# A hybrid decoder layer: the residual x transposed on TensorE from the copy already on chip, a reordered front, and half of the low parts of one normalised input computed on GpSimd

## Chip, cores and metric

The kernel runs on one core of one Trainium2 chip. The metric is the device time of one execution in microseconds (us), as the median over several executions. A core has five engines that run side by side and wait for one another only through semaphores: TensorE (PE in the profile), VectorE (DVE), ScalarE (ACT), GpSimd (POOL) and SyncE (SP). Sixteen DMA engines move data between the memory of the chip (HBM) and the buffers on the core.

## What is computed

One inference step of one layer, for a prompt of 256 tokens and for 8 single sample tokens (264 token columns in all), with model width 2048:

```
n1 = rmsnorm(x) ; [q | f | v | g | u] = n1 @ w_in            # 2048 -> 5120
o  = rmsnorm(hgrn2(q, f, v)) * silu(g)                       # 8 heads, state 128x128
pm = multiscale_pool(u) @ w_pool
h  = x + [o | pm] @ w_out                                    # the residual x is added here
h  = h + (silu(gate) * up) @ w_down                          # FFN on rmsnorm(h) @ w_gate_up, width 5632
h  = h + sigmoid(h @ w_ple_gate) * rmsnorm(p @ w_ple)
y  = rmsnorm(h)
```

The new recurrent states and the last 15 pooling inputs are outputs as well. All is float32.

## The kernel before

Activations are kept with features on the 128 partitions and the 264 tokens along the row, one tile of 128x264 for each 128 features (`KT = 16` tiles for the width). Each float32 operand of a product is split into two float16 parts, high and low, and each 128x128 piece of weights is multiplied three times: high by high, high by low, low by high (lines 1415, 1417 and 1419, in `stream`). A weight **block** is 512 KB, two tiles of 128 input features by 512 outputs. For each block SyncE issues the load into one of four `raw` buffers when the block four before it has been split (`load`, line 410, waiting for `lo_done`), ScalarE makes the high part (`split`, line 531), VectorE the low part (line 798), and TensorE runs 24 matmuls over it. The order on every engine is written out by hand by block number `b`. The input projection is blocks 0 to 79 in ten groups of eight; each group ends with the eviction of four accumulator tiles (`evict_in`, lines 540, 950, 951 and 955), and TensorE may write a tile of the next group only when `acc_free` says that it was evicted.

Small products and transposes are **jobs**: a numbered list `JOBS` in which each uses the next of four PSUM banks (`wrk`), and `job(name)` makes TensorE wait until the job four before it has been taken out (`drained`). Their instructions are woven between the matmuls of a block.

**The front.** x is loaded token by token (`x_tok`, two loads of 1 MB by SyncE, semaphores `x_in`), the sample rows `x_smp` and the identity matrix `ident` by ScalarE's queue. TensorE runs matmuls on zeros (`idle_matmuls`, line 1442, their counts in `IDLE_MMS`), transposes the sample rows (line 1450), sums their squares (`xq`, line 1456), transposes the gain vectors (`vec`, line 1459), and transposes the scaled x (`n1_k`, lines 1468 and 1470). VectorE sums half of the squares of each x tile (`half_squares`, line 854), takes the sample results (lines 859 to 861), forms the reciprocal roots (lines 864 to 869, 816 to 818) and scales x (line 888).

**The residual x.** The features-on-partitions copy of x, needed in `h_all` when the output projection begins, comes from a second load of x: 32 loads of 64 KB by GpSimd's queue (line 504), paced by `lo_done`, into `x_blk`, and eight VectorE 32x32 block transposes of 128x512 (line 1218) in blocks 33 to 40. GpSimd also loads the recurrent states (line 471, from `lo_done` 8 on), the pooling buffer, and fills scratch with zeros (lines 493 to 496).

**Before the FFN.** When h is complete, VectorE forms each of the 16 tiles of the normalised h (line 1239, `ntmp`, four temporaries), ScalarE its high part (line 732), and VectorE its low part (line 1246). VectorE then waits in tile k for the low part of tile k - 4. The FFN follows in 22 groups of 8 blocks. ScalarE splits blocks 4 to 7 of the FFN's group 0 and 0 to 3 of group 1 after the last high part, and evicts group 0 (line 540) after these.

## Time and profile before

| | |
|---|---|
| median of 3 executions | 1227.67 us (1224.66 to 1231.83) |
| profiled execution: its own time, its span | 1222.89 us, 1221.1 us |
| TensorE busy in the span | 1196.5 us (98%) |
| VectorE, ScalarE, GpSimd busy | 793.4 us, 589.5 us, 48.7 us |
| mean granted TensorE clock | 0.992 of full speed |
| HBM traffic | 192 GB/s over the span |

Times in the rows are us from the start of the span. A matmul's row tells its latency; matmuls overlap, so the rate is read from the distance of their starts. In a timeline row the square brackets tell how long the engine had been idle and which instruction's end released it. A granted clock of 1.00 is 2.4 GHz, one of 0.50 is 1.2 GHz.

### The profile page before, as it was taken

To read this page: it belongs to the slowest core of one execution; us is meant where nothing else is said; L and a number is where in the kernel's file an instruction comes from. 1 tells how busy PE (TensorE), PEld (TensorE's weight loads), DVE (VectorE), ACT (ScalarE), POOL (GpSimd) and SP (SyncE) were. 2 spreads that over 40 slices of the span, in tenths; PEclk is the share of its full clock that TensorE was granted. 3 is DMA by queue.
4 is the path that set the end of the run, shared out by engine and by line. 5 is a ranking of instruction groups with operands and counts; after the bars stand their busy time and mean duration, and the time that the engine had idled before them with its cause. 6 is when DMAs were issued, how large, how long until landed. Compare 5 with 4: busy or idle time off the path is not lost.

```text
span 1221.1 us, 27627 instructions
## 1 busy us (share of the span) xinstructions
PE 1196.5 (98%) x10779; PEld 1042.5 (85%) x10779; DVE 793.4 (65%) x1169; ACT 589.5 (48%) x727; POOL 48.7 (4%) x73
## 2 busy tenths in 40 slices
PE   7999999999999899999999999999999999999996
PEld 6888989888888788888888888888888888888885
DVE  6677787678868865665656556565664645454786
ACT  5543533555546745555545554555453434343442
POOL 2430110100000000000000000000000000000000
PEclk8999999999999999999999999999999999999998
DMA  7885765766555566575665757657464646565551
GB/s 236 247 247 143 238 182 167 222 183 202 176 204 191 172 194 219 158 222 170 210 202 170 222 158 223 189 182 226 142 242 144 235 159 221 172 221 184 189 162 72
DMA packets 173336, 234.98 MB, mean 192 GB/s; under 512 B 10690, under 2 KB 111273, under 8 KB 173000
## 3 DMA queue, kind: packets, MB, share of 16 engines
q1 hardware_dynamic: 167728, 220.30, 55.9%
q0 software_dynamic: 4048, 12.19, 3.6%
q10 hardware_dynamic: 1504, 1.70, 0.4%
q8 instruction: 39, 0.64, 0.2%
q14 instruction: 17, 0.14, 0.0%
HBM read 227.18 MB, written 7.43 MB: 192 GB/s over the span
## 4 chain that ended last, share of the span: by engine, by line
PE 88%; DVE 6%; DMA 3%; ACT 2%; issue 2%; ACTq 0%; SPq 0%; DVEq 0%
PE acc L1415 28%; PE acc L1419 28%; PE acc L1417 28%; DVE lo L798 2%; PE wrk L1561 2%; DMA raw<-in_w_in_dram 1%; ACT hi L531 1%; DMA ident<-in_c_ident_dram 1%; DMA raw<-in_w_gate_up_dram 0%; PE wrk L1442 0%; DVE nrm L1246 0%; DMA raw<-in_w_out_dram 0%; DVE a L1239 0%; DVE tg L1239 0%; PE wrk L1768 0%
## 5 line engine op out<-in xcount | busy, mean ns | idle before, releaser
L1415 PE MATMUL acc<-nrm,hi 128*128 128x264 f16 x2304 | 636.7, 276 | 7.1 <-DVE tg L1252 2.6
L1417 PE MATMUL acc<-nrm,hi 128*128 128x264 f16 x2304 | 636.7, 276 | 0.0
L1419 PE MATMUL acc<-nrm,lo 128*128 128x264 f16 x2304 | 636.6, 276 | 0.0
L798 DVE SCALAR_TENSOR_TENSOR lo<-raw,hi 128x1024 f16<-128x1024 f32 x414 | 497.1, 1221 | 213.2 <-ACT hi L531 209.5
L531 ACT ACTIVATE hi<-raw 128x1024 f16<-128x1024 f32 x414 | 424.1, 1051 | 327.6 <-DMA raw<-in_w_gate_up_dram 105.7
L1415 PEld LDWEIGHTS acc<-nrm,hi 128*128 128x128 f16 x2304 | 227.4, 99 | 41.4 <-DVE tg L1252 2.9
L1419 PEld LDWEIGHTS acc<-nrm,lo 128*128 128x128 f16 x2304 | 228.4, 99 | 32.7
L1417 PEld LDWEIGHTS acc<-nrm,hi 128*128 128x128 f16 x2304 | 228.4, 99 | 32.6
L1415 PE MATMUL acc<-big,hi 128*128 128x264 f16 x720 | 198.7, 276 | 0.0
L1417 PE MATMUL acc<-big,hi 128*128 128x264 f16 x720 | 198.7, 276 | 0.0
L1419 PE MATMUL acc<-big,lo 128*128 128x264 f16 x720 | 198.7, 276 | 0.0
L540 ACT ACTIVATE gate_t<-acc 128x264 f32<-128x264 f32 x84 | 32.7, 391 | 154.9 <-PE acc L1419 154.9
L1252 DVE SCALAR_TENSOR_TENSOR tg<-acc,gate_t 128x264 f32<-128x264 f32 x44 | 19.0, 433 | 111.8 <-ACT gate_t L540 111.8
L1417 PEld LDWEIGHTS acc<-big,hi 128*128 128x128 f16 x720 | 70.5, 98 | 10.7
L1415 PEld LDWEIGHTS acc<-big,hi 128*128 128x128 f16 x720 | 70.5, 98 | 10.6
L1419 PEld LDWEIGHTS acc<-big,lo 128*128 128x128 f16 x720 | 70.5, 98 | 10.5
L1415 PE MATMUL acc<-mix,hi 128*128 128x264 f16 x256 | 70.6, 276 | 1.1 <-DVE mix L1129 0.7
L1419 PE MATMUL acc<-mix,lo 128*128 128x264 f16 x256 | 70.7, 276 | 0.0
L1417 PE MATMUL acc<-mix,hi 128*128 128x264 f16 x256 | 70.7, 276 | 0.0
L1561 PE MATMUL wrk<-big 128*128 128x64 f32 x224 | 32.2, 247 | 0.6 <-DVE mix L1014 0.6
L1561 PEld LDWEIGHTS wrk<-big 128*128 128x128 f32 x224 | 31.7, 190 | 1.1 <-DVE mix L1014 0.9
L1415 PEld LDWEIGHTS acc<-mix,hi 128*128 128x128 f16 x256 | 25.0, 98 | 5.4 <-DVE lo L798 1.0
(287 smaller groups left out, 747.4 us busy)
## 6 DMA issues: line engine op xcount, KB each, us to landing
raw<-in_w_gate_up_dram SPq DMA_DIRECT2D x352, 256.0 KB, 3.8
raw<-in_w_down_dram SPq DMA_DIRECT2D x88, 512.0 KB, 4.7
raw<-in_w_in_dram SPq DMA_DIRECT2D x80, 512.0 KB, 4.5
raw<-in_w_out_dram SPq DMA_DIRECT2D x32, 512.0 KB, 4.4
raw<-in_w_ple_gate_dram SPq DMA_DIRECT2D x32, 512.0 KB, 4.7
state<-in_state_hgrn_dram POOLq DMA_DIRECT2D x8, 512.0 KB, 6.1
out_new_hgrn_sample_dram<-state POOLq DMA_DIRECT2D x8, 512.0 KB, 5.2
xe<-in_x_prompt_dram SPq DMA_DIRECT2D x2, 1024.0 KB, 6.9
```

Source lines behind the costliest of these rows:

```text
L531: nc.scalar.activation(hi[:, st.hl_slot(j), :], raw[:, st.raw_slot(j), :], ACT.Copy, scale=WSCALE).then_inc(hi_done, 1)
L540: nc.scalar.activation(gate_t[:, n, :], acc[:, n, 0:TOK], ACT.Sigmoid, scale=c).then_inc(gate_ready, 1)
L798: stt(lo[:, st.hl_slot(j), :], raw[:, st.raw_slot(j), :], WSCALE, hi[:, st.hl_slot(j), :], ALU.mult, ALU.subtract).then_inc(lo_done, 1)
L1252: stt(tg32[:, n, :], acc[:, n, 0:TOK], C_FFN, gate_t[:, n, :], ALU.mult, ALU.mult).then_inc(acc_free, 1)
L1415: mm(out, wh, x_hi[:, kt, :], start=first, stop=False)
L1417: mm(out, wh, x_lo[:, kt, :], start=False, stop=False)
L1419: last = mm(out, wl, x_hi[:, kt, :], start=False, stop=final)
L1561: last = mm(out[:, n * 64:(n + 1) * 64].rearrange("p (n k) -> p n k", k=1 << l), k, right, start=True, stop=True)
```

## The change

Three edits are made together. First, the second load of x and the VectorE transposes are removed; TensorE transposes `x_tok` in blocks 8 to 15 (jobs `xt_0` to `xt_15`, two 128x128 transposes each), and ScalarE copies each 128x256 result into `h_all`. The buffers on top of `x_tok` may be filled only after the last of these, so GpSimd's load of the pooling buffer and its memsets now wait for `xt_15` in place of `n1_15`. Second, in the front, ScalarE's queue issues the load of `ident` ahead of that of `x_smp`, which is written without the split into four columns, and the counts of the matmuls on zeros are 26, 4, 0 and 12 where they were 24, 16, 8 and 16. Third, the low parts of the odd tiles before the FFN are made by GpSimd, which signals `n_odd`; VectorE keeps the even ones.

```diff
-X_TURN_AT, X_LOAD_AT, PT_AT, CONST_AT = 33, 4, 16, 4
+X_AT, PT_AT, CONST_AT = 8, 16, 4
-IDLE_MMS = (24, 16, 8, 16)
+IDLE_MMS = (26, 4, 0, 12)
...
+    if _b in range(X_AT, X_AT + KT // 2):
+        JOBS += [(f"xt_{2 * (_b - X_AT) + _n}", "act") for _n in range(2)]
...
-            pool.wait_ge(drained["dve"], drain_of(f"n1_{KT - 1}")[1])
+            pool.wait_ge(drained["act"], drain_of(f"xt_{KT - 1}")[1])
             pool.dma_start(buf_tok, io["state_pool"][0].rearrange("b j c -> (b j) c")).then_inc(buf_in, 16)
...
-            pool.wait_ge(masks_ready, 1)
-            for m in range(SEQ // 32):
-                for q in range(4):
-                    if q % 2 == 0:
-                        pool.wait_ge(lo_done, X_LOAD_AT + AHEAD + 2 * m + q // 2)
-                    src = io["x_prompt"][0, 32 * m:32 * m + 32, :].rearrange("r (k q f) -> r k q f", q=4, f=32)
-                    pool.dma_start(x_blk[32 * q:32 * q + 32, :, 32 * m:32 * m + 32], src[:, :, q, :]).then_inc(x_blk_in, 16)
...
+            for k in range(1, KT, 2):
+                pool.wait_ge(n_hi_ready, KT + k + 1)
+                pool.wait_ge(xn_ready, X_SCALED + k + 1)
+                nc.gpsimd.tensor_tensor(n_lo[:, k, :], ntmp(k), n_hi[:, k, :], ALU.subtract).then_inc(n_odd, 1)
...
-            act.dma_start(x_smp.rearrange("b (c d) -> b c d", c=4), io["x_sample"][:, 0, :].rearrange("b (c d) -> b c d", c=4))\
-                .then_inc(x_in[2], 16)
             act.dma_start(ident[:], io["c_ident"]).then_inc(id_in, 16)
+            act.dma_start(x_smp, io["x_sample"][:, 0, :]).then_inc(x_in[2], 16)
...
+            def x_tile(k):
+                wait_job(f"xt_{k}")
+                nc.scalar.activation(h_all[:, k, 0:SEQ], wrk[:, JOB[f"xt_{k}"] % JOB_BANKS, 0:SEQ], ACT.Copy)\
+                    .then_inc(drained["act"], 1)
...
                 if b + AHEAD > len(EARLY_SPLITS):
                     split(*MIX_BLOCKS[b + AHEAD])
+                if b in range(X_AT, X_AT + KT // 2):
+                    for n in range(2):
+                        x_tile(2 * (b - X_AT) + n)
...
-                if b in range(X_TURN_AT, X_TURN_AT + KT // 2):
-                    ks = slice(2 * (b - X_TURN_AT), 2 * (b - X_TURN_AT) + 2)
-                    dve.wait_ge(x_blk_in, 16 * 4 * (SEQ // 32))
-                    nc.vector.transpose(h_all[:, ks, 0:SEQ], x_blk[:, ks, :]).then_inc(x_ready, 1)
...
                     if k >= 4:
-                        dve.wait_ge(n_ready, k - 3)
+                        dve.wait_ge(n_odd if k % 2 else n_ready, k // 2 - 1)
...
-                if k >= 2:
+                if k >= 2 and k % 2 == 0:
                     dve.wait_ge(n_hi_ready, KT + k - 1)
                     tt(n_lo[:, k - 2, :], ntmp(k - 2), n_hi[:, k - 2, :], ALU.subtract).then_inc(n_ready, 1)
...
+            def x_features(k):
+
+                out = job(f"xt_{k}")
+                nc.tensor.transpose(out[:, 0:P], x_tok[:, 0, k * P:(k + 1) * P], ident[:])
+                yield
+                nc.tensor.transpose(out[:, P:SEQ], x_tok[:, 1, k * P:(k + 1) * P], ident[:]).then_inc(job_done, 1)
+                yield
...
-                stream(S_FFN, i, n_hi, n_lo, ready=lambda j: pe.wait_ge(n_ready, 2 * j + 2))
+                stream(S_FFN, i, n_hi, n_lo, ready=ffn_ready)
```

On TensorE, the start of the program, before (`hi` holds the zeros of the matmuls that do no work, `xe` the sample rows, `mix` the sums of squares, `big` the gain vectors):

```order
L1442 MATMUL wrk<-hi 128x264 x24
L1450 MATMUL wrk<-ident,xe 128x8 x16
L1442 MATMUL wrk<-hi 128x264 x16
L1456 MATMUL wrk<-mix,ones 128x8
L1442 MATMUL wrk<-hi 128x264 x8
L1459 MATMUL wrk<-ident,big 128x81
L1442 MATMUL wrk<-hi 128x264 x16
```

and the same place in the changed program:

```order
L1443 MATMUL wrk<-hi 128x264 x26
L1451 MATMUL wrk<-ident,xe 128x8 x16
L1443 MATMUL wrk<-hi 128x264 x4
L1457 MATMUL wrk<-mix,ones 128x8
L1460 MATMUL wrk<-ident,big 128x81
L1443 MATMUL wrk<-hi 128x264 x12
```

The matmuls on zeros ahead of the sums of squares went from 16 to 4, those ahead of the vectors from 8 to none.

On TensorE, the start of block 8 in the changed program (before, the same place is matmuls of lines 1415, 1417 and 1419 alone):

```order
L1416 MATMUL acc<-nrm,hi 128x264
L1699 MATMUL wrk<-ident,xe 128x128
L1418 MATMUL acc<-nrm,hi 128x264
L1701 MATMUL wrk<-ident,xe 128x128
L1420 MATMUL acc<-nrm,lo 128x264
L1699 MATMUL wrk<-ident,xe 128x128
L1416 MATMUL acc<-nrm,hi 128x264
L1701 MATMUL wrk<-ident,xe 128x128
```

Four transposes of x were woven into the block; each of blocks 8 to 15 has four.

On VectorE, the tiles from 8 on before the FFN (`a` and `tg` are the temporaries, `nrm` the low parts; `lo<-raw,hi` is the split of a weight block), before:

```order
L798 SCALAR_TENSOR_TENSOR lo<-raw,hi 128x1024
L1239 SCALAR_TENSOR_TENSOR a<-hid,gf,wrk 128x264
L1246 TENSOR_TENSOR nrm<-tg,nrm 128x264
L1239 SCALAR_TENSOR_TENSOR a<-hid,gf,wrk 128x264
L1246 TENSOR_TENSOR nrm<-tg,nrm 128x264
L1239 SCALAR_TENSOR_TENSOR tg<-hid,gf,wrk 128x264
L1246 TENSOR_TENSOR nrm<-a,nrm 128x264
L1239 SCALAR_TENSOR_TENSOR tg<-hid,gf,wrk 128x264
L1246 TENSOR_TENSOR nrm<-a,nrm 128x264
```

and in the changed program:

```order
L803 SCALAR_TENSOR_TENSOR lo<-raw,hi 128x1024
L1240 SCALAR_TENSOR_TENSOR a<-hid,gf,wrk 128x264
L1247 TENSOR_TENSOR nrm<-tg,nrm 128x264
L1240 SCALAR_TENSOR_TENSOR a<-hid,gf,wrk 128x264
L1240 SCALAR_TENSOR_TENSOR tg<-hid,gf,wrk 128x264
L1247 TENSOR_TENSOR nrm<-a,nrm 128x264
L1240 SCALAR_TENSOR_TENSOR tg<-hid,gf,wrk 128x264
```

For each two tiles one subtraction has left VectorE; eight stand at the end of GpSimd's program.

## Rows read from the trace of the kernel before

**Rows 1.** The page, busy time of each engine.
```profile
PE 1196.5 (98%) x10779; PEld 1042.5 (85%) x10779; DVE 793.4 (65%) x1169; ACT 589.5 (48%) x727; POOL 48.7 (4%) x73
```

**Rows 2.** Waits of TensorE, whole span: us in total, times, longest us.
```profile
PE acc L1415 <- DVE tg L1252: 2.6, 1, 2.6
PE acc L1415 <- DVE big L955: 1.6, 1, 1.6
...
PE wrk L1561 <- DVE mix L1014: 0.6, 1, 0.6
...
PE acc L1415 <- DVE big L951: 0.5, 1, 0.5
```

**Rows 3.** Timeline of the front: start us, us, engine, line, operation.
```profile
9.27 1.87 PE L1450 MATMUL wrk<-ident,xe 8*128 8x8 f32 x16 [3.69 <-DMA ident<-in_c_ident_dram]
9.41 1.06 ACT L569 ACTIVATE big<-xe 128x1024 f32<-128x1024 f32 x1 [1.88 <-DMA xe<-in_x_prompt_dram]
...
11.07 3.70 PE L1442 MATMUL wrk<-hi 128*128 128x264 f16 x16
...
12.20 1.21 DVE L854 CUSTOM_DVE_ANT_0 big<-xe 128x1024 f32<-128x1024 f32 x1
...
15.03 0.17 DVE L864 TENSOR_SCALAR gate_t<-wrk 128x8 f32<-128x8 f32 x1 [1.61 <-PE wrk L1456]
...
17.37 0.49 DVE L888 TENSOR_SCALAR big<-xe,gate_t 128x512 f32<-128x512 f32 x1
```

**Rows 4.** DMA queue of ScalarE (q10) from 0 to 2.5, then from 5 to 6.
```profile
q10 hardware_dynamic: 7, 0.06, 10.1%
...
q10 hardware_dynamic: 27, 0.01, 4.6%
```

**Rows 5.** Window: stretch, length, busy PE PEld DVE ACT POOL, PEclk, DMA share, GB/s.
```profile
45.00:50.00 5.00, 3.39 (x31) 2.77 (x29) 3.86 (x7) 1.34 (x2) 4.72 (x9) 1.00 1.02 308
```

**Rows 6.** Timeline of TensorE inside block 1, woven transposes.
```profile
24.33 0.27 PE L1470 MATMUL wrk<-ident,big 128*128 128x128 f32 x1
...
24.44 0.28 PE L1419 MATMUL acc<-nrm,lo 128*128 128x264 f16 x1
```

**Rows 7.** Timeline of GpSimd, VectorE and ScalarE, 40 to 54 us.
```profile
40.90 0.97 POOL L493 MEMSET mix<- 128x1024 f32 x1
41.79 1.83 POOL L494 MEMSET xe<- 128x2048 f16 x1
...
41.16 0.17 DVE L921 TENSOR_TENSOR lbt<-lbt 128x8 f32<-128x8 f32 x1
41.36 2.41 DVE L922 TENSOR_SCALAR lbt<-lbt 128x8 f32<-128x8 f32 x1
...
44.01 2.36 DVE L798 SCALAR_TENSOR_TENSOR lo<-raw,hi 128x1024 f16<-128x1024 f32 x2
...
53.11 1.06 ACT L531 ACTIVATE hi<-raw 128x1024 f16<-128x1024 f32 x1 [6.50 <-DMA raw<-in_w_in_dram]
```

**Rows 8.** Timeline of VectorE near 162 us.
```profile
162.36 0.70 DVE L1218 STREAM_TRANSPOSE hid<-big 128x512 f32<-128x512 f32 x1
```

**Rows 9.** Timeline of VectorE, then ScalarE, before the FFN.
```profile
400.75 0.48 DVE L1239 SCALAR_TENSOR_TENSOR a<-hid,gf,wrk 128x264 f32<-128x264 f32 x1
401.15 0.42 DVE L1246 TENSOR_TENSOR nrm<-tg,nrm 128x264 f16<-128x264 f32 x1
...
405.95 0.48 DVE L1239 SCALAR_TENSOR_TENSOR tg<-hid,gf,wrk 128x264 f32<-128x264 f32 x1
...
393.69 0.82 ACT L732 ACTIVATE nrm<-a 128x264 f16<-128x264 f32 x2 [0.88 <-DVE a L1239]
...
408.20 3.90 ACT L531 ACTIVATE hi<-raw 128x1024 f16<-128x1024 f32 x4
```

**Rows 10.** Windows at the change from FFN group 0 to 1.
```profile
424.00:425.00 1.00, 0.82 (x5) 0.59 (x6) 0.86 (x4) 1.00 (x1) 0.00 (x0) 0.65 0.82 251
...
427.00:428.00 1.00, 1.00 (x8) 0.72 (x7) 1.00 (x2) 1.00 (x2) 0.00 (x0) 0.65 0.24 84
```

More of the change, by code:

```diff
@@ L268, in build @@
         e_sq, e_ssq = mix[:, 0:TOK], mix[:, TOK:2 * TOK]
-        x_blk = big[:, 4 * HEADS * TOK:4 * HEADS * TOK + KT * SEQ].rearrange("p (k t) -> p k t", t=SEQ)
         y_tok = big[:, 0:2 * D].rearrange("p (a d) -> p a d", a=2)
@@ L348, in build @@
         xs_ready, ns_hi = sem("xs_ready"), sem("ns_hi")
-        x_blk_in, masks_ready, x_ready = sem("x_blk_in"), sem("masks_ready"), sem("x_ready")
         sq_ready, mean_ready, rstd_ready, xn_ready = sem("sq_ready"), sem("mean_ready"), sem("rstd_ready"), sem("xn_ready")
-        n_hi_ready, n_ready = sem("n_hi_ready"), sem("n_ready")
+        n_hi_ready, n_ready, n_odd = sem("n_hi_ready"), sem("n_ready"), sem("n_odd")
         q16_ready, s_hi_ready, s_lo_ready = sem("q16_ready"), sem("s_hi_ready"), sem("s_lo_ready")
@@ L917, in constants @@
                 nc.vector.tensor_copy(ident16[:], ident[:])
-                nc.vector.tensor_copy(masks[:], masks_f).then_inc(masks_ready, 1)
+                link(nc.vector.tensor_copy(masks[:], masks_f))
                 link(nc.vector.reciprocal(lbt[:, 2, :], lbt[:, 1, :]))
@@ L1151, in _ @@
                     if st is S_OUT_O[0]:
-                        dve.wait_ge(x_ready, KT // 2)
+                        dve.wait_ge(drained["act"], drain_of(f"xt_{KT - 1}")[1])
                     out_tiles(st, S_OUT_O.index(st))
@@ L1698, in in_jobs @@
                     yield from ple_features()
+                if b in range(X_AT, X_AT + KT // 2):
+                    for n in range(2):
+                        yield from x_features(2 * (b - X_AT) + n)
                 for c in range(QUADS):
@@ L1753, in _, with ffn_ready @@
             stream(S_PLE, 0, pt_hi, pt_lo, ready=sum_h, layout=lambda j, n, kk: (kk * COLS + n * P, kk))
+            def ffn_ready(j):
+                pe.wait_ge(n_ready, j + 1)
+                pe.wait_ge(n_odd, j + 1)
             with pe.Fori(0, S_FFN.groups) as i:
-                stream(S_FFN, i, n_hi, n_lo, ready=lambda j: pe.wait_ge(n_ready, 2 * j + 2))
+                stream(S_FFN, i, n_hi, n_lo, ready=ffn_ready)
             out = job("es")
@@ L1776, in y_transposes @@
                 yield
-            stream(S_GATE, 0, n_hi, n_lo, ready=lambda j: pe.wait_ge(n_ready, KT + 2 * j + 2))
+            stream(S_GATE, 0, n_hi, n_lo, ready=lambda j: pe.wait_ge(n_ready, KT // 2 + 2 * j + 2))
             with pe.Fori(1, S_GATE.groups - 1) as i:
```

## Prediction

> **What bounds the kernel now.** I read the page first: TensorE is busy 98% of the span [rows 1], so a change is worth only what it adds to TensorE's work or takes from its few waits, and what the clock does around them. Then the list of TensorE's waits: apart from the front, those that this change can touch are 2.6 us at the end of the FFN's first group, 1.6 and 0.5 us at the ends of the first two groups of the input projection, and 0.6 us at the second diagonal [rows 2]. The timeline of the front shows where the first 17 us go, and windows show the granted clock.
>
> The front: TensorE waits 3.69 us for the identity matrix and starts the sample transposes at 9.27; the 16 matmuls on zeros behind them take 3.70 us, 0.23 each where one of the same shape takes 0.11 later [rows 6], which is the lower clock, so that VectorE, done with its squares at 13.41, waits 1.61 us for the sums of squares and starts its chain at 15.03; x is scaled from 17.37 on [rows 3].
>
> The first group change: a VectorE instruction on 8 columns took 2.41 us, from 41.36 to 43.77, until a GpSimd memset of 1.83 us (41.79 to 43.62) had ended; the two weight splits behind it ran until 46.37 and the evictions that TensorE waited for came after them [rows 7].
>
> The FFN: the last product tile starts at 405.95, ScalarE starts the four splits of group 0 at 408.20, everything behind them is late, TensorE waits 2.6 us for the first eviction [rows 9, 2], and the clock is at its lower level behind it. A mean of 0.65 is 0.3 at full speed and 0.7 at half, so from 424.3 to 427.7, 3.4 us [rows 10].
>
> **The change part by part.** All terms are in us against the profiled execution, 1222.9 (span 1221.1). It lies 4.8 below the median of the three timed runs, 1227.67; I take the difference over unchanged.
>
> *Transposes of x on TensorE.* 32 instructions. In block 1 the same kind, woven, starts 0.11 before the matmul behind it [rows 6], so each takes one slot of 0.11: 32 x 0.11 = **+3.5**. No wait hides them, since the block loop runs without a gap. Their 16 copies on ScalarE are 128x256 from PSUM; two tiles of 128x264 take it 0.82 from SBUF [rows 9], so about 6.6 in some 25 us in which ScalarE idles up to 6.5 at a time [rows 7]: nothing. What is queued behind a copy is the split of the block five ahead, with four blocks of 2.7 us in hand.
>
> *The second load and VectorE's transposes go.* ScalarE sat 6.50 idle for a weight block that landed at 53.11 [rows 7], with states, pooling buffer, x and weights on the DMA engines at once. Without x, and with the pooling buffer and memsets put behind block 15, the 2.41 us instruction should take what its neighbours take (about 0.2), and both splits and evictions move up by 2.2, more than the 1.6 of wait: **-1.6**. The 0.5 of the second group change is late by a weight block that lands late: **-0.5**. The 0.6 at the diagonal ends a fully occupied stretch of VectorE in which block transposes of 0.70 stand, the last at 162.36 [rows 8]; two of them make 1.3: **-0.6**. Zero to 2.7 is the bound of the three together. GpSimd's buffer loads and memsets now start about 2 us after the last copy, near 70, and its zeros are first needed in block 18, near 74. If VectorE meets the memset again there, it costs it up to 2.2, in a place where it has two blocks (5.3) in hand: nothing.
>
> *The front.* Four matmuls on zeros in place of 16 take 0.9 (3.70 / 16 x 4) and end at about 12.0, ahead of VectorE. So VectorE's chain starts when its squares are done, at 13.41: -1.6. That is the lower bound. The upper one comes from the identity matrix. It was issued at 1.39, second in its queue, and landed at 9.27. Of that queue 7 packets with nearly all of the 64 KB of sample rows had moved by 2.5 us, while the small packets of the identity move only after 5 [rows 4]: what was issued first went at once, what came second waited behind the first 1 MB of x. Issued first it should land near 6.5, and the sample rows (8 packets) near 7. Then the sample work is over before the second half of x lands at 9.41 [rows 3], VectorE's squares run 9.41 to 10.6 instead of 12.20 to 13.41, nothing waits, and scaling starts at 17.37 - 1.61 - 2.8 = 13.0: -4.4. Against this stands the clock. With fewer matmuls on zeros TensorE has little to do between the last of them and the first weight block: eight transposes, one microsecond with a gap on each side. Before, it was down after 3.69 of idle time [rows 3]. If it falls here at the first block and stays at 1.2 GHz for 3.4 us, as after 424 [rows 10], that costs 1.7, and twice that if it stays twice as long. Of 4.4 I keep **-3.1**.
>
> *The low parts.* From product to low part VectorE takes 0.40, and the seven pairs from tile 8's product to tile 15's 5.20, 0.74 each, so a low part is 0.34 [rows 9]. Two tiles took 1.48, now 1.14. Up to tile 8 ScalarE's splits set the pace (I find 0.3 to gain there). From tile 8 to the end of tile 15, 400.75 to 406.35, the 5.6 become 8 x 0.40 + 4 x 0.34 = 4.6. Together **-1.4** on ScalarE's last high part, on the four splits behind it, and on loads, gates and evictions that follow from them. TensorE's wait becomes 1.2 of 2.6. The wait of 1.6 at the first group change left the clock at full speed [rows 5], and that of 2.6 did not: I expect the fall to go. It cost half of the 3.4 us: **-1.7**. GpSimd's subtraction of 128x264 is in no row. Its memset moves 2048 columns in 1.83 [rows 7], 0.24 for 264; one pass for each operand and the result gives 0.7. Between 0.24 and that I take 0.7. It has 1.14 for each tile and two tiles of slack through `ntmp`, so VectorE does not wait for it.
>
> The Trainium skill (GPSIMD Engine Reference, Performance versus the Vector engine) gives 4497 ns for this operation on 2048 columns; by that figure a tile is an estimated 0.58, and the sum would be the same.
>
> **Sum.** 3.5 - 1.6 - 0.5 - 0.6 - 3.1 - 1.4 - 1.7 = -5.4. That is 1217.5 in the profiled execution's terms, **1222.3** as a median, 0.44% faster. 0.5% (6.1 us) is about what a measurement of this kernel can tell from no change.
>
> **The rivals.**
>
> *A. The clock holds in the front.* Then the front gives its 4.4 and the sum is -6.7: 1221.0, faster. For it: the wait of 1.6 at 45 to 47 did not lower the clock [rows 5]. Against it: two gaps follow each other closely here.
>
> *B. The identity does not land earlier,* because both loads share the DMA engines with 2 MB of x. The front gives 1.6, the sum is -3.9: 1223.8. The packets of [rows 4] speak against it.
>
> *C. GpSimd and VectorE hold each other up.* The instruction that ended with the memset [rows 7] shows that it can happen. VectorE would then do its own 4.6 plus four subtractions of 0.7 where 5.6 stood: 1.8 later instead of 1.4 earlier, with the clock's fall kept, so -5.4 + 3.2 + 1.7: 1227.2, no change. Against it: the instruction just before the one held up, a two-input one at 41.16, took 0.17 while another memset ran, from 40.90 to 41.87 [rows 7].
>
> By the Trainium skill (GPSIMD Engine Reference, Specifications) contention is to be expected with VectorE instructions that have two SBUF inputs, as line 1246 and the weight split have. The 0.17 us neighbour does not agree with that, though it is a short one and a memset reads nothing.
>
> *D. The DMA engines stay behind,* as the states alone keep weight blocks late. ScalarE's copies stand behind a split that waits for the block four ahead, so TensorE would meet full banks from block 10 on: block 12 landed at 53.1 and TensorE would want the first bank back near 52. The waits of 1.6 and 0.5 become others of that size and one or two us are added: -5.4 + 2.1 + 1.5 = -1.8, 1225.9.
>
> *E. Slower: GpSimd is the bound before the FFN.* VectorE's tile 15 needs GpSimd's low part of tile 11, its sixth, and the first can begin at about 394.1, when ScalarE has made the first two high parts [rows 9]. With T for one, tile 15 starts no earlier than 394.1 + 6 T. It is level with before (405.95) at T = 2.0; the rest of the sum (-2.3) is eaten up at T = 2.4, and from 3.4 on the kernel is 6 us slower: 1234. That is five times my 0.7.
>
> **How the numbers follow.** My forecast has 0.46, A 0.19, B 0.10, C 0.09, D 0.07, E and anything like it 0.09. Within the forecast the clock's cost in the front may be anything between its two levels, 1.2 to each side, so 0.4 of it lies beyond 6.1 us. Faster: 0.19 + 0.4 x 0.46 = 0.37, with what is left of noise in the median 0.39. Slower: E, 0.09. Within 0.5%: 0.52. The range goes from A less the uncertainty of the median (the three runs lie 7 apart, so their median may be off by 2 to 3) at 1218 to a little beyond C at 1229. The forecast's own is 1220 to 1225.
>
> **What would show it.** The sample transposes start at or before 7.5 instead of 9.27; VectorE's x scaling near 13; no TensorE wait at the first two group changes and none near 167; the block loop from 8 to 15 longer by 3.5; GpSimd's subtractions under 1.1 apart; ScalarE's four splits near 1.4 earlier relative to the first product tile; a wait near 1.2 at the end of FFN group 0 with the clock at 1.00 behind it. I am wrong if the identity lands at 9 again, if VectorE waits for `n_odd`, if a fall of the clock at the first weight blocks eats the front, or if TensorE waits on full banks in blocks 10 to 15.

## The result, and the profile after

| | before | changed |
|---|---|---|
| median | 1226.81 us (5 runs, 1222.43 to 1231.83) | 1218.66 us (5 runs, 1217.32 to 1219.73) |
| ratio of the times, 95% interval | | 0.9939 (0.991 to 0.9969) |
| profiled execution: time, span | 1222.89, 1221.1 us | 1218.66, 1216.9 us |

The medians lie 8.1 us apart; the measured ratio of the times is 0.9939, 0.61% or 7.5 us faster. The two profiled executions differ by only 4.2 us of span, and much of what follows is about the other 4. The page, busy time, answers to [rows 1]: TensorE 3.0 us more, VectorE 8.1 and GpSimd 14.9 less.

```profile
PE 1199.5 (99%) x10789; PEld 1045.2 (86%) x10789; DVE 785.3 (65%) x1153; ACT 594.0 (49%) x743; POOL 33.8 (3%) x49
```

TensorE's waits (total, times, longest), to be held against [rows 2]: 2.6 has become 1.1, and the two group changes and the diagonal have left the list. In the front the sample rows have taken the identity's place.

```profile
PE wrk L1451 <- DMA xe<-in_x_sample_dram: 1.8, 1, 1.8
PE acc L1416 <- DVE tg L1253: 1.1, 1, 1.1
```

Timeline of the front of the changed kernel (start, us, engine, line, operation, idle before), beside [rows 3]:

```profile
7.72 1.06 ACT L566 ACTIVATE big<-xe 128x1024 f32<-128x1024 f32 x1 [4.43 <-DMA xe<-in_x_prompt_dram]
8.06 1.30 PE L1451 MATMUL wrk<-ident,xe 8*128 8x8 f32 x16 [1.79 <-DMA xe<-in_x_sample_dram]
10.19 1.06 ACT L566 ACTIVATE big<-xe 128x1024 f32<-128x1024 f32 x1 [1.31 <-DMA xe<-in_x_prompt_dram]
13.84 0.49 DVE L893 TENSOR_SCALAR big<-xe,gate_t 128x512 f32<-128x512 f32 x1
17.39 0.38 PE L1416 MATMUL acc<-nrm,hi 128*128 128x264 f16 x1 [0.74 <-DVE nrm L915]
```

x is scaled 3.5 earlier (17.37 to 13.84), although its halves arrive later (10.19 against 9.41). The windows of the same execution (length, busy PE PEld DVE ACT POOL, granted clock, DMA share, GB/s) show the price: TensorE, idle from about 6.3 to 8.06, drops to the lower clock near the end of the window 8 to 9 and stays there for over 13 us, through the first weight blocks.

```profile
8.00:9.00 1.00, 0.94 (x14) 0.97 (x15) 1.00 (x2) 0.87 (x2) 0.00 (x0) 0.90 0.98 363
...
10.00:16.00 6.00, 5.08 (x23) 3.57 (x22) 5.55 (x19) 4.47 (x9) 2.94 (x5) 0.50 1.05 374
16.00:22.00 6.00, 5.26 (x26) 3.65 (x25) 5.96 (x12) 5.82 (x10) 0.00 (x0) 0.50 0.67 189
22.00:23.00 1.00, 1.00 (x9) 0.78 (x8) 1.00 (x1) 0.00 (x0) 0.00 (x0) 0.77 0.71 182
```

The first group change, beside [rows 7]: the instruction on 8 columns takes 0.17 where it took 2.41, and ScalarE's copies of x (line 662) run between the splits.

```profile
40.47 0.17 DVE L927 TENSOR_SCALAR lbt<-lbt 128x8 f32<-128x8 f32 x1
...
40.88 2.36 DVE L803 SCALAR_TENSOR_TENSOR lo<-raw,hi 128x1024 f16<-128x1024 f32 x2
...
47.02 0.64 ACT L662 ACTIVATE hid<-wrk 128x256 f32<-128x256 f32 x2
```

Before the FFN, beside [rows 9]: GpSimd's subtractions, 1.14 apart with 0.39 idle between them; VectorE beside them; ScalarE's four splits, at 406.05 where they were at 408.20.

```profile
401.38 0.75 POOL L518 TENSOR_TENSOR nrm<-a,nrm 128x264 f16<-128x264 f32 x1 [0.39 <-ACT nrm L737]
402.52 0.76 POOL L518 TENSOR_TENSOR nrm<-tg,nrm 128x264 f16<-128x264 f32 x1 [0.39 <-ACT nrm L737]
...
401.51 0.48 DVE L1240 SCALAR_TENSOR_TENSOR tg<-hid,gf,wrk 128x264 f32<-128x264 f32 x1
401.91 0.48 DVE L1240 SCALAR_TENSOR_TENSOR a<-hid,gf,wrk 128x264 f32<-128x264 f32 x1
402.31 0.42 DVE L1247 TENSOR_TENSOR nrm<-tg,nrm 128x264 f16<-128x264 f32 x1
402.65 0.48 DVE L1240 SCALAR_TENSOR_TENSOR a<-hid,gf,wrk 128x264 f32<-128x264 f32 x1
...
406.05 3.90 ACT L529 ACTIVATE hi<-raw 128x1024 f16<-128x1024 f32 x4
```

Windows behind FFN group 0, of the changed kernel: the clock holds.

```profile
420.00:425.00 5.00, 3.88 (x35) 3.14 (x34) 4.08 (x8) 4.96 (x7) 0.00 (x0) 1.00 0.84 267
425.00:430.00 5.00, 5.00 (x47) 4.36 (x45) 4.72 (x6) 2.44 (x3) 0.00 (x0) 1.00 0.58 162
```

The same two windows of the kernel before had 0.93 and 0.73:

```profile
420.00:425.00 5.00, 2.37 (x19) 1.69 (x18) 3.94 (x7) 4.58 (x6) 0.00 (x0) 0.93 0.72 213
425.00:430.00 5.00, 5.00 (x34) 3.82 (x33) 4.70 (x7) 4.24 (x5) 0.00 (x0) 0.73 0.54 169
```

Three stretches between fixed points of TensorE's program carry all the rest. They are read from one profiled execution of each kernel, as the starts of the first weight matmul of block 8, of the first of block 24, and of the very last weight matmul; "waits" are TensorE's at the first and second group change, and "clock" tells whether the granted clock fell behind the second, with what that cost. The experiments that are described below are in it too.

| execution | to block 8 | block 8 to 24 | block 24 to last | waits | clock |
|---|---|---|---|---|---|
| before, first profile | 46.9 | 50.4 | 1110.5 | 1.6, 0.5 | held |
| before, second profile (12) | 47.3 | 55.1 | 1110.0 | 1.6, 3.5 | fell, 1.7 |
| 1, front alone | 42.7 | 54.3 | 1109.8 | 1.6, 2.6 | fell, 1.7 |
| 2, x on TensorE alone | 45.7 | 53.3 | 1109.3 | 0, 0 | held |
| 3, odd low parts alone | 46.2 | 52.0 | 1107.0 | 1.6, 2.1 | held |
| 8, before, memsets later | 46.9 | 55.4 | 1108.2 | 0, 3.5 | fell, 1.7 |
| changed, first profile | 44.1 | 53.3 | 1106.3 | 0, 0 | held |
| changed, second profile (5) | 41.0 | 53.3 | 1106.7 | 0, 0 | held |
| 9, changed, x loaded as well | 42.8 | 53.3 | 1106.0 | 0, 0 | held |
| 11, changed, no odd low parts | 42.5 | 53.3 | 1109.4 | 0, 0 | held |

The table's points are worked out by counting matmuls on `acc`, eight blocks being 192 of them. The last column is read from windows of the clock. Three of them, of 70 to 80 us, are of the kernel before (first profile), of its second profile, and of experiment 8; 0.83 of ten microseconds is 3.4 us at half speed, 1.7 us of work lost:

```profile
70.00:80.00 10.00, 10.00 (x91) 8.81 (x89) 8.20 (x12) 5.24 (x5) 3.15 (x5) 1.00 0.89 254
...
70.00:80.00 10.00, 7.40 (x52) 5.95 (x53) 7.82 (x15) 5.78 (x9) 3.91 (x6) 0.83 0.92 239
...
70.00:80.00 10.00, 7.38 (x52) 6.17 (x53) 8.20 (x16) 4.94 (x9) 5.35 (x9) 0.83 0.99 259
```

Experiment 1 has 0.94 in 60 to 70 and 0.89 in 70 to 80, again 1.7 lost. With this the middle column adds up for the kernels without the transposes: 50.4, plus what the wait exceeds 0.5 by, plus 1.7 where the clock fell, gives 55.1, 54.2, 52.0 and 55.1 where 55.1, 54.3, 52.0 and 55.4 were measured (experiment 8 has one more wait there, of 0.2).

### The profile page after: what moved, and what is told of

The parts are those of the page before. It is cut to its first block, busy times and chain, and to the rows that moved or that the text cites. A ratio compares the mean times of both kernels' runs of the same rounds, so it can differ in the third digit from the quotient of the medians.

```text
span 1216.9 us, 27632 instructions
## 1 busy us (share of the span) xinstructions
PE 1199.5 (99%) x10789; PEld 1045.2 (86%) x10789; DVE 785.3 (65%) x1153; ACT 594.0 (49%) x743; POOL 33.8 (3%) x49
## 4 chain that ended last, share of the span: by engine, by line
PE 94%; DVE 2%; ACT 1%; DMA 1%; issue 1%; ACTq 0%; SPq 0%; DVEq 0%
PE acc L1416 30%; PE acc L1418 30%; PE acc L1420 30%; PE wrk L1562 2%; DVE lo L803 1%; DMA raw<-in_w_gate_up_dram 1%; ACT hi L529 1%; DMA xe<-in_x_sample_dram 1%; PE wrk L1547 0%; DVE a L1240 0%; PE wrk L1536 0%; PE wrk L1785 0%; PE wrk L1691 0%; ACT big L773 0%; PE wrk L1511 0%
```

## The experiments

The first four were compared on one chip (kernel before: 1224.53, 28 runs), 5 to 8 on another occasion (1224.80, 15 runs), 9 to 12 on a third (1223.91, 13 runs).

**1 to 3: each part of the change alone.** The edits are the diff of the change in three pieces.

```diff
-IDLE_MMS = (24, 16, 8, 16)                          # 1: with the order of the two loads
+IDLE_MMS = (26, 4, 0, 12)
...
+    if _b in range(X_AT, X_AT + KT // 2):            # 2: with everything of xt_* and x_blk
+        JOBS += [(f"xt_{2 * (_b - X_AT) + _n}", "act") for _n in range(2)]
...
+            for k in range(1, KT, 2):                # 3: with everything of n_odd
```

> The kernel before with the front's edit alone (order of the two loads on ScalarE's queue, 26, 4, 0 and 12 matmuls on zeros). Theory 1 (the first weight matmul comes about 3.4 us earlier, and the clock, at its lower level until about 22 us, takes some 2.2 of it back): first weight matmul near 17.4, block 8 reached 1.0 to 1.3 us earlier than before. Rival (the front does nothing, all of the 8 us between the medians comes from elsewhere): block 8 at the same time as before. Second rival (with a clock that happens to hold, the front is worth its 3.4): block 8 3.4 earlier. Medians: 1.2 faster, 0, 3.4 faster.

Measured: 1220.56 (1217.46 to 1222.17, 11 runs), ratio 0.9964 (0.9949 to 0.9979), by the ratio 4.4 us faster. In its profile the sample transposes start at 7.47 and block 8 comes 4.2 earlier than before. The clock was at 0.50 from 11 to 14 only, and full before the first weight matmul:

```profile
10.00:11.00 1.00, 0.58 (x4) 0.47 (x5) 1.00 (x1) 1.00 (x2) 0.79 (x2) 0.85 1.05 387
11.00:14.00 3.00, 2.67 (x13) 1.52 (x10) 2.69 (x15) 2.05 (x6) 2.16 (x4) 0.50 1.05 387
14.00:15.00 1.00, 0.94 (x8) 0.88 (x8) 1.00 (x2) 1.00 (x3) 0.00 (x0) 0.94 1.08 402
```

Theory 1 had the clock wrong; the second rival, block 8 3.4 earlier, came nearest. Part of it was lost again in this execution: the wait at the second group change was 2.6, and the clock fell behind it.

> The kernel before with the transposes of x on TensorE and without the second load, nothing else of the change. Theory 1 (a trade that is level): +3.5 for 32 transposes, -1.6, -0.5, -0.6 and some tenths for waits that go: 0.5 to 0.8 us slower to no change in one profile. Rival (the second load costs more in most executions than in the profiled one of before, where executions lie 9 us apart, and its absence is where the narrow spread of the changed kernel comes from): 3 to 5 us faster in the median and a spread under 3 us.

Measured: 1222.40 (1220.99 to 1223.85, 11 runs), ratio 0.9988 (0.9976 to 0.9999). Both group waits and the diagonal's are gone, 3.3 us of transposes are there, and the wait of 2.1 at the FFN still brings a clock of 0.66 in 425 to 430. The gain lies between theory and rival. What stands out is the spread: 2.9 us over 11 runs, where experiments 1 and 3, which keep the second load, spread over 4.7 and 5.3 in 11, and the kernel before over 7.4 in 28.

> The kernel before with the odd low parts on GpSimd alone. Theory 1: ScalarE's last high part 1.4 us earlier against the first product, with the wait at the end of the FFN's first group near 1.2 us instead of 2.6 and no fall of the clock behind it: 3.1 to 3.4 us faster, in the profile and in the median. Rival (the fall of the clock behind that wait is chance, and would have been absent anyway): 1.4 faster in the median.

Measured: 1221.73 (1220.23 to 1225.51, 11 runs), ratio 0.9988 (0.9974 to 1.0002); the last stretch of the table is 3.5 shorter than before, the FFN wait 0.5, the clock 1.00 behind it. So this profile bears out the theory, but the ratio, 1.5 us with an interval from none to 3.2, does not tell its 3.1 to 3.4 from the rival's 1.4; experiment 11 is the better evidence. By the ratios the three savings, 4.4 + 1.5 + 1.5 = 7.4, add up to the 0.61% that the whole change saved, within an uncertainty of 1.4 to 1.8 each.

**4 to 7: the clock and the order in the front.** All are the changed kernel; 4, 6 and 7 run more matmuls on zeros, so that TensorE has no long gap. 5 is the changed kernel once more.

```diff
-IDLE_MMS = (26, 4, 0, 12)
+IDLE_MMS = (42, 12, 0, 26)                          # 4, 6, 7
...
             act.dma_start(x_smp, ...)               # 6: ahead of ident again
             sp.dma_start(ident[:], io["c_ident"])   # 7: on SyncE's queue, ahead of x
```

> The changed kernel with 42, 12, 0 and 26 matmuls on zeros in place of 26, 4, 0 and 12, so that TensorE has work in all of the front. Theory 1 (idle time in the front lets the clock fall, and that costs 2.2 us of the first weight blocks): clock at 1.00 from 5 us on, first weight matmul near 17.4 or some tenths later, block 8 2 us earlier than in the changed kernel, median 2 us faster. Rival (the clock falls whatever TensorE does there): same clock, the additional zeros at the lower rate run until 16 to 17 us and push the first weight matmul 1 to 2 us later.

Measured: 1216.77 (1215.85 to 1218.21, 6 runs), ratio 0.9942 (0.9918 to 0.9967). The clock is 1.00 in all of the front, the first weight matmul starts at 16.6 and block 8 at 41.0, 3.0 earlier than in the changed kernel's first profile. In the front the theory came out; what the zeros are worth is seen only against experiment 5.

> The changed kernel as it is, on the same chip as the next three. Theory 1: it repeats 1217 to 1220 us, and lies 2 us above the kernel with more matmuls on zeros (1216.8) where the clock falls in the front. Rival (the difference between the two is one of chips): both within 0.5 us.

Measured: 1215.97 (1215.71 to 1216.29, 5 runs), ratio 0.9934 (0.992 to 0.9947). The theory missed: experiment 4 is not 2 us faster than this. The same program has block 8 at 41.0 without any extra zeros. In this execution the clock fell just as before, but came back at 15 and not at 22.5:

```profile
8.00:9.00 1.00, 1.00 (x13) 0.93 (x13) 0.65 (x2) 0.44 (x2) 0.00 (x0) 0.66 0.93 350
9.00:14.00 5.00, 4.37 (x19) 2.59 (x17) 4.62 (x18) 3.13 (x6) 2.94 (x5) 0.50 1.05 385
...
15.00:16.00 1.00, 0.64 (x5) 0.40 (x3) 0.89 (x3) 1.00 (x3) 0.00 (x0) 0.93 0.96 279
16.00:24.00 8.00, 7.27 (x65) 6.55 (x66) 7.96 (x14) 7.15 (x13) 0.00 (x0) 1.00 0.74 211
```

From the first weight matmul to block 8 it is 24.3 us here and 26.7 in the first profile. So the price of the clock in the front is not a constant of the program: 2.4 us in one execution, nothing in another. Experiments 10 and 11, with the same front, had it at 0.50 until just before 20 and took 25.8 to 25.9. Experiment 9 had it back at 14 and lost it again from 17.3 to 20.7, just behind its first weight matmul, and took 26.0.

> The changed kernel with 42, 12, 0 and 26 matmuls on zeros, and the sample rows loaded ahead of the identity again, as before. Theory 1 (what is issued second waits behind the first half of x, so the order is worth the time from the sample rows' landing near 7.1 to 8.1 to that of the identity near 9.3): sample transposes at 9.3 and scaling of x at 14.5 to 15.8 instead of 13 to 13.8, 1.5 to 2.5 us slower than with the identity first. Rival (VectorE's squares of the second half of x set the time in either order, and that half lands earlier, near 9.1, when the sample rows are first): under 0.5 us between them.

Measured: 1218.22 (1217.73 to 1219.22, 5 runs), ratio 0.9954 (0.994 to 0.9968), 2.2 over experiment 5 and 2.0 over experiment 7, with ranges that don't touch. The order of the two loads, with the sample rows written in four columns again, is all that sets it apart from experiment 4, which ran on another chip: by the ratios 1.5 us, and block 8 at 42.8 against 41.0. The identity, second in its queue, landed at 9.62, and x was scaled at 15.06:

```profile
9.62 1.15 PE L1452 MATMUL wrk<-ident,xe 8*128 8x8 f32 x16 [1.39 <-DMA ident<-in_c_ident_dram]
...
15.06 0.49 DVE L894 TENSOR_SCALAR big<-xe,gate_t 128x512 f32<-128x512 f32 x1
```

> The changed kernel with 42, 12, 0 and 26 matmuls on zeros, the identity issued by SyncE ahead of x, and the sample rows by ScalarE: neither comes second in a queue. Theory 1 (each queue's first load goes at once): sample transposes near 6.5, second half of x 0.4 us later than otherwise, scaling of x from 12.5 to 13.5, that is 0 to 1 us earlier than with both on ScalarE's queue. Rival (a load of 128 small packets ahead of x holds up x itself): halves of x 1 us later or more, and the kernel slower by that.

Measured: 1216.23 (1215.85 to 1216.91, 5 runs), ratio 0.9937 (0.9923 to 0.995): level with experiment 5. Its clock was 1.00 in all of the front and x was scaled at 13.00, though the sample transposes started at 7.50, right behind the zeros, and not at 6.5. Yet no gain over the unchanged program shows; whether extra zeros pay on a chip whose clock comes back late wasn't compared.

**8: the kernel before with its memsets some 5 us later.**

```diff
+            pool.wait_ge(lo_done, 11)
             nc.gpsimd.memset(scores[:, 0:2], 0.0)
```

> The kernel before, with GpSimd's memsets waiting for the low part of weight block 10, so that they no longer run beside VectorE's constants; the second load of x follows them. Theory 1 (the memset holds up the VectorE instruction of 2.41 us and so the evictions): that instruction takes 0.2 us, and the wait of 1.6 us at the first group change is gone. Rival (the DMA traffic of the second load of x causes it): the wait stays. The second group change keeps its wait of 0.5 to 2.6 us in either case, since weight blocks land late.

Measured: 1225.86 (1223.34 to 1228.58, 10 runs), ratio 1.0012 (0.9998 to 1.0025). The wait at the first group change is gone and the 8-column instruction takes 0.17, so the memset was its cause; the second load can't be, as its first transfer is issued behind the memsets in the kernel before (43.66). The time didn't follow, for two reasons that this one execution shows. The clock, full in that place in the kernel before, fell behind the first weight matmul (0.66, 0.50, 0.50 and 0.64 in the four windows from 21 to 25, 1.7 us lost), so that block 8 came at 46.9 as before; and the second change cost its wait of 3.5 and a second fall. Whether either goes with the moved memsets was not tested. VectorE's evictions and splits ran at their usual 0.43 and 1.23 beside the moved memset (the split only for its first 0.3 us):

```profile
46.93 1.81 POOL L495 MEMSET xe<- 128x2048 f16 x1
...
43.20 0.17 DVE L923 TENSOR_SCALAR lbt<-lbt 128x8 f32<-128x8 f32 x1
...
47.55 0.43 DVE L956 SCALAR_TENSOR_TENSOR big<-acc,gate_t 128x264 f32<-128x264 f32 x1 [0.24 <-ACT gate_t L541]
48.49 1.23 DVE L799 SCALAR_TENSOR_TENSOR lo<-raw,hi 128x1024 f16<-128x1024 f32 x1 [0.51 <-ACT hi L532]
```

**9: the changed kernel with the blocked load of x put back.** The loaded copy isn't used.

```diff
+            pool.wait_ge(masks_ready, 1)
+            for m in range(0, 6):                   # and 6, 7 behind the memsets
...
+                    pool.dma_start(x_blk[...], src[:, :, q, :]).then_inc(x_blk_in, 16)
```

> The changed kernel with the 32 transfers of the second, blocked load of x put back on GpSimd's queue, gated as before; the transposes stay on TensorE and the loaded copy of x isn't used. Theory (the second load costs through the DMA engines, which then have no time to spare between 50 and 80 us, so that the weight blocks come late): the DMA share of the stretches 50:60 and 60:70 rises from 0.79 and 0.39 to about 1.0, TensorE waits again at the second group change by 0.5 to 3.5 us (the four kernels with that load waited 0.5, 2.6, 2.1 and 4.0 there), and block 8 to block 24 takes 54 to 57 us instead of 53.3; the median is 1 to 3 us over the changed kernel's 1216 to 1218.7. Rival (the waits at the group changes came of the order on VectorE and ScalarE, or of GpSimd's memsets alone, and not of the load): no wait there, 53.3 us from block 8 to block 24, no change within 0.5 us.

Measured: 1216.77 (1215.4 to 1218.46, 4 runs), ratio 0.9947 (0.9929 to 0.9964). The expectation's wait of 4.0 for experiment 8 should read 3.5. My theory was half wrong. The DMA engines did fill up (1.02 in 50 to 60, 0.97 in 60 to 70), and weight blocks took longer from issue to landing. This is the DMA view of 44 to 72 us, its last column the median us to landing; first the changed kernel:

```profile
raw<-in_w_in_dram SPq DMA_DIRECT2D x9, 512.0 KB, 4.4
```

then experiment 9:

```profile
raw<-in_w_in_dram SPq DMA_DIRECT2D x9, 512.0 KB, 7.6
big<-in_x_prompt_dram POOLq DMA_DIRECT2D x16, 64.0 KB, 5.9
```

and the kernel before, second profile:

```profile
raw<-in_w_in_dram SPq DMA_DIRECT2D x10, 512.0 KB, 9.5
big<-in_x_prompt_dram POOLq DMA_DIRECT2D x22, 64.0 KB, 6.7
```

But TensorE didn't wait, and block 8 to 24 took the same 53.3. Late weights alone don't make the wait. The first profile of the kernel before had 8.8 in this view and waited 0.5, experiment 1 had 7.9 and waited 2.6. The likely reason why experiment 9 with its 7.6 waited for nothing is that TensorE, with 3.3 us of transposes in blocks 8 to 15, came to each block later. That is an inference: weights were also less late here than in any of the five executions of the other kernels with that load (7.9 to 9.5), and the memsets lay elsewhere.

**10 and 11: GpSimd's share before the FFN,** three times over, and none.

```diff
+                for _ in range(2):                  # 10: ahead of the subtraction that counts
+                    links += 1
+                    nc.gpsimd.tensor_tensor(n_lo[:, k, :], ntmp(k), n_hi[:, k, :], ALU.subtract).then_inc(n_rep, 1)
+                    pool.wait_ge(n_rep, links)
...
-            for k in range(1, KT, 2):               # 11: with everything of n_odd
```

> The changed kernel with each of GpSimd's eight subtractions done three times over, one after the other, so that its step is about 2.3 us and the distance between two of its tiles about 3.4 instead of 1.14 us where it is busy throughout. Rival E of the prediction (GpSimd the bound): the last of the eight ends near 393.8 + 7 x 3.4 + 2.3 = 420 instead of 405.5, the wait ahead of FFN group 1 grows from 1.1 to 10 us or more or waits appear within group 0, the clock falls behind it, and the kernel is 8 us or more slower than the changed one. If FFN group 0 takes the tiles as slowly as they come (21.6 us for 16 tiles, an odd one each 2.7 us), much of it is hidden: 2 to 5 us slower. Rival (VectorE's eight remaining subtractions and the products set the pace, GpSimd has room): the time stays within 1 us.

Measured: 1222.10 (1220.97 to 1223.5, 10 runs), ratio 0.9988 (0.9976 to 0.9999). From tile 7 to tile 13 a step of three took 2.24 us and steps followed one another without a gap, so the distance was 2.24, not my 3.4; a step that met a weight split of VectorE's took 3.1. VectorE now stood idle 0.58 in each pair of tiles for GpSimd, and TensorE met a weight block that wasn't split, 3.9 us, with the clock at 0.83 in 410 to 420:

```profile
407.50 0.49 DVE L1246 SCALAR_TENSOR_TENSOR tg<-hid,gf,wrk 128x264 f32<-128x264 f32 x1 [0.58 <-POOL nrm L524]
...
412.51 0.40 PE L1422 MATMUL acc<-nrm,hi 128*128 128x264 f16 x1 [3.91 <-DVE lo L809]
```

By the ratios this is 5 to 6.6 us over the changed kernel (0.9947 of experiment 9, 0.9934 of 5), between the two figures I had given, and about level with the kernel before.

The profile of this experiment also shows what the changed kernel's doesn't: the two engines do hold each other up. The first two are GpSimd's passes, one that met a split and one beside which VectorE did nothing; the others are VectorE's split and subtraction beside passes of GpSimd.

```profile
393.65 1.55 POOL L524 TENSOR_TENSOR nrm<-a,nrm 128x264 f16<-128x264 f32 x1
...
409.28 0.68 POOL L524 TENSOR_TENSOR nrm<-a,nrm 128x264 f16<-128x264 f32 x1
...
392.96 1.70 DVE L809 SCALAR_TENSOR_TENSOR lo<-raw,hi 128x1024 f16<-128x1024 f32 x1 [0.30 <-ACT hi L535]
...
396.21 0.88 DVE L1253 TENSOR_TENSOR nrm<-a,nrm 128x264 f16<-128x264 f32 x1
```

The split takes 1.23 alone and the subtraction 0.37 to 0.42. Four subtractions took 0.85 to 0.88, three passes 1.55. So part of what this experiment cost is contention, and not GpSimd's rate alone.

> The changed kernel with all 16 low parts back on VectorE. Theory: the wait ahead of FFN group 1 is 2.1 to 2.6 us instead of 1.1, the clock falls behind it as in the kernel before (0.65 to 0.93 in stretches of 5 us), and the kernel takes 2.5 to 3.5 us more than the changed one. Rival (the odd low parts gave the wait of 1.4 us alone, and the clock's fall hung on something else): 1.0 to 1.6 us more, with the clock at 1.00 behind the wait.

Measured: 1218.78 (1216.44 to 1219.99, 4 runs), ratio 0.9956 (0.994 to 0.9973). The wait is 2.4 and the clock 0.78 and 0.88 behind it; the last stretch of the table is 2.7 to 3.4 longer than with the odd low parts. Theory right.

```profile
420.00:425.00 5.00, 3.46 (x22) 2.61 (x23) 4.08 (x8) 4.96 (x7) 0.00 (x0) 0.78 0.85 258
425.00:430.00 5.00, 5.00 (x41) 4.16 (x40) 4.58 (x6) 2.51 (x3) 0.00 (x0) 0.88 0.66 189
```

**12: the kernel before, unchanged, a second profile.**

> The kernel before, unchanged, for a second profile. Theory (the second load of x leaves the DMA engines no room, so that what lands last at the second group change differs from one execution to the next): the wait at the second group change isn't 0.5 again but somewhere in 0.5 to 3.5 us, while the wait at the first (1.6, set by the memset beside VectorE's small operation) and the one behind FFN group 0 (2.6) come back within 0.1. Rival: all three come back within 0.1, and the spread of the kernel's time comes from elsewhere.

Measured: this execution took 1227.57, its span 1225.7, 4.6 over the first profile. The waits are 3.5, 1.6 and 2.8 (second change, first change, FFN; the last 0.2 over its first value and not within 0.1). ScalarE stood idle 3.29 for a block of weights, and VectorE's gates came behind its split; the lines are of ScalarE, VectorE and TensorE:

```profile
69.48 1.06 ACT L531 ACTIVATE hi<-raw 128x1024 f16<-128x1024 f32 x1 [3.29 <-DMA raw<-in_w_in_dram]
...
70.57 1.23 DVE L798 SCALAR_TENSOR_TENSOR lo<-raw,hi 128x1024 f16<-128x1024 f32 x1 [3.12 <-ACT hi L531]
...
72.60 0.27 PE L1415 MATMUL acc<-nrm,hi 128*128 128x264 f16 x1 [3.54 <-DVE big L951]
```

Block 8 to 24 took 55.1 instead of 50.4: 4.6 again, so this one stretch holds the whole difference between the two executions of the same program. The wait makes 3.0 of it and the clock, which fell behind it, the other 1.7.

## Why the prediction was right, and where it wasn't

The range held the time, though only just: 1218.7 lies 0.7 above its lower end and below the forecast's own 1220 to 1225. At 0.61% the change is past the line of 0.5%, a side to which the prediction gave 0.39 against 0.52 for staying within it. The mechanisms of the likeliest case were all there, one of them badly undersized. The sum of -5.4 was set against the profiled execution; there it came to -4.2. (The low parts, 1.04 and 0.3, make 1.3 and not 1.4; nothing hangs on it.) Term by term:

| term | predicted | first profiles | what the runs add |
|---|---|---|---|
| transposes on TensorE | +3.5 | +3.3 | the same in nine executions |
| first group change | -1.6 | -1.6 | 8: the memset was its cause |
| second group change | -0.5 | -0.5 | waits of 2.1 to 3.5 in four other executions, with 1.7 of clock in three of them |
| diagonal | -0.6 | -0.6 | |
| front | -3.1 | -1.2 | -4.2 in experiment 1; the clock takes 0 to 2.4 back |
| low parts | -1.4 | -1.5 | |
| clock behind FFN group 0 | -1.7 | -1.7 | 11: both together 2.7 to 3.4 |

In the third column the front is the stretch to block 8 less the 1.6 of wait. The low parts are the FFN's wait, 2.6 to 1.1; the clock is what the windows of 420 to 430 lost before, 5 x 0.07 + 5 x 0.27. With the diagonal they make 3.8 of the 4.2 by which the last stretch is shorter; the other 0.4 is a wait on `hid` (line 1137) that the first profile of the changed kernel happens not to have, and its second has with 0.8.

**The term that was mis-sized** is "The 0.5 of the second group change is late by a weight block that lands late: -0.5". The reason was right, the number was one draw of a quantity that varies, and the clock was left out of it. In the five executions of kernels that load x twice and keep the transposes off TensorE, this wait was 0.5, 2.1, 2.6, 3.5 and 3.5 us, and behind the last three the clock fell, for another 1.7. The stretch lost 0.5, 2.1, 4.3, 5.2 and 5.2 us by both, and the profile that I had happened to show the least. I had seen that it lay 4.8 under the median of the timed runs and took "the difference over unchanged"; the difference was in the main this wait with its clock, and the change removes both. This is where the 8.1 of the medians comes from when the profiles show 4.2, as far as two profiles of one program and three of its near relatives can tell; the untraced runs weren't looked into.

With it falls the sentence "No wait hides them, since the block loop runs without a gap", for most executions. Block 8 to 24 takes 53.3 with the transposes, always, and 50.4 to 55.4 without. The change exchanges a cost of changing size for work of fixed size. Experiment 9 fits this: the load was back, the weights were later again, and TensorE was as quick. What the exchange brings is evenness (a spread of 2.9 us in experiment 2).

**The front** came out by its steps: the identity issued first no longer held anything up, 4 zeros ended before VectorE's squares, and x was scaled near 13 (13.84 and 13.18 in the changed kernel, 12.99 to 13.34 in experiments 1 and 9 to 11). One was missed: the sample rows, now second, landed at 8.0 in the first profile and not at 7, and both halves of x came 0.8 to 1.3 later there. In all seven profiles with the identity first on ScalarE's queue ScalarE takes up the second half of x at 9.76 to 10.19, in the six with the sample rows first at 9.13 to 9.55. Rival B is refuted by experiment 6, in which the identity as second load landed at 9.62 and cost 1.5 to 2.2 us. Rival A, a clock that holds, is false as it stands, since the clock fell in every profile of the changed front with its 26, 4, 0 and 12 zeros; but its price, nothing lost, occurred all the same, in experiments 1 and 5. What the fall cost between the first weight matmul and block 8 was 2.4, 1.7, 1.6, 1.6, 0.2 and 0, by when the clock came back and whether it fell again. I gave it a fixed price in the middle of its bounds; both ends occurred.

**Before the FFN** GpSimd's subtraction was put at 0.7 and took 0.69 to 0.76. Rival C did not happen: in the changed kernel VectorE's products and subtractions start 0.40 and 0.34 after one another, exactly as alone. That is owed to timing, and the prediction didn't see it. Each pass of GpSimd's starts 0.2 us into a subtraction of VectorE's, runs beside products, which took 0.48 as ever, and ends before the next subtraction or split. Where the passes are three times as long, VectorE's subtractions take 0.85 to 0.88 and its splits up to 1.70 (experiment 10). The Trainium skill (GPSIMD Engine Reference, Specifications) has contention to be expected with VectorE instructions of two SBUF inputs; subtraction and split have two, and experiment 10's rows agree. Rival E was tested at T = 2.24, where the prediction had the whole kernel level with before from 2.4 on; it measured 0.9988 of it, contention included. That the clock's fall here goes with the length of the wait is borne out by thirteen executions, all but experiment 10: it fell behind waits of 2.1, 2.1, 2.4, 2.6 and 2.8 us and stayed at 1.00 behind 0.5, 0.7, 0.7, 0.8, 0.9, 1.1, 1.7 and 2.0. The last is experiment 8's, whose last stretch is short for that reason (1108.2). The two sides touch, so the length alone doesn't settle a wait near 2: at the second group change the clock held behind 2.1 (experiment 3) and fell behind 2.6, 3.5 and 3.5. Rival D (full banks in blocks 10 to 15) didn't occur; ScalarE took its copies in pairs of 0.64, and the weights arrived in 4.4 us.

## What to carry to other kernels

Before a wait that ends with a DMA is priced from one profile, compare that execution's time with the timed runs: if it lies at the edge of their range, the wait in it is a draw, and a second profile of the same program costs less than the mistake. Price the clock with the wait. Where the DMA engines are full, removing traffic pays through the waits it ends, and these exist only as far as the consumer is ahead; work put on TensorE in the same place may then cost little. Shortening a wait behind which the clock falls can be worth more than its length: here 1.5 us of wait brought 3. And if a second engine is put to work beside a first without slowing it, look at which instructions actually ran side by side before calling them independent.

## What the hardware showed

- GpSimd's memset of 128x2048 float16 held up one kind of VectorE instruction, a 128x8 `tensor_scalar`, to 2.41 us in all four executions where the two met, and left `scalar_tensor_tensor` of 128x264 and 128x1024 at 0.43 and 1.23 beside it (experiment 8). Why the one was held, no run here shows.
- GpSimd's two-input subtraction of 128x264 and VectorE's two-input instructions held each other up where they ran side by side (experiment 10): VectorE's subtraction 0.85 to 0.88 instead of 0.42, its weight split up to 1.70 instead of 1.23, GpSimd's pass 1.55 instead of 0.68. VectorE's product of line 1240, which reads `wrk` in PSUM, kept its 0.48.
- One program's clock fell between 8 and 9 us in two executions, and came back at 15 in one and at 22.5 in the other.
- Two small loads on one queue: the first moved at once, the second waited behind megabytes of another queue. The identity was in use by 7.3 to 8.1, with the sample rows, when it was first, and at 9.3 to 9.8 when second.
- A pass of GpSimd over 128x264 float32 with a float16 operand and result took 0.69 to 0.76 us in the changed kernel, against 0.34 from start to start on VectorE.
